# The norm's factor moved from in front of a feed-forward block to its gate and its result, in two of four blocks of a float32 transformer kernel

## What is computed

```python
def rms_norm(x, g, eps):
    xf = x.astype(jnp.float32)
    y = xf * lax.rsqrt(jnp.mean(xf * xf, axis=-1, keepdims=True) + eps)
    return (y * g.astype(jnp.float32)).astype(x.dtype)

def swiglu(h, w_gate_up, w_down):
    gu = h @ w_gate_up
    g, u = jnp.split(gu, 2, axis=-1)
    return (jax.nn.silu(g) * u) @ w_down

def second_block(...):
    for l in range(DEPTH):                       # DEPTH = 2
        ...
        x = x + rms_norm(m, norm_mix_post[l], NORM_EPS)
        h = rms_norm(x, norm_ffn_pre[l], NORM_EPS)
        f = swiglu(h, w_gate_up[l], w_down[l])
        x = x + rms_norm(f, norm_ffn_post[l], NORM_EPS)
```

## Time and profile before

| | |
|---|---|
| median of 3 runs | 4113.35 us (4108.27 to 4121.14) |
| the profiled execution, own time | 4109.69 us |
| its span | 4107.9 us |
| PE busy | 3872.9 us, 94% |
| DVE, ACT, POOL busy | 1541.3, 1503.3, 1261.4 us |
| mean granted TensorE clock | 0.973 of full |

### The profile page before, as it was taken

One profiled execution on the slowest core, in us unless ns is written; L12 is line 12 of the kernel. 1 busy time (PEld: TensorE's weight loads), 2 busy tenths in 40 slices (PEclk: granted clock), 3 DMA queues, 4 the chain that ended last, 5 costly groups with the idle time before them and its releaser, 6 DMA issues.

```text
span 4107.9 us, 59148 instructions
## 1 busy us (share of the span) xinstructions
PE 3872.9 (94%) x22684; PEld 3081.7 (75%) x22684; DVE 1541.3 (38%) x2360; ACT 1503.3 (37%) x2506; POOL 1261.4 (31%) x524
## 2 busy tenths in 40 slices
PE   6998999999986999999979999989998999998998
PEld 4875678888874777788857778868886777876886
DVE  2023454242423555353335555331115655323112
ACT  3324343121234444332245555232224555333222
POOL 2530042222221000244432323434442322343443
PEclk9999999999998999999999999999999999999999
DMA  4324621111120000122222122222221221222222
GB/s 179 114 93 147 243 88 62 62 62 62 62 67 31 16 15 20 67 87 97 97 73 67 62 67 72 97 68 97 97 97 62 67 67 62 79 94 74 98 93 87
DMA packets 84707, 333.87 MB, mean 81 GB/s; under 512 B 9520, under 2 KB 9648, under 8 KB 78000
## 3 DMA queue, kind: packets, MB, share of 16 engines
q1 hardware_dynamic: 83808, 329.22, 23.6%
q10 hardware_dynamic: 720, 2.10, 0.1%
HBM read 329.18 MB, written 2.10 MB: 81 GB/s over the span
## 4 chain that ended last, share of the span: by engine, by line
PE 62%; issue 26%; POOL 6%; DVE 3%; ACT 2%; POOLq 0%; DVEq 0%; ACTq 0%
PE pB L1903 13%; PE pB L276 12%; PE pB L278 12%; PE pB L277 12%; POOL w_lo L2423 6%; PE pO L1517 2%; PE pS L408 2%; PE pB L1499 1%; PE pS L1499 1%; PE pT L1509 1%; PE pS L1933 1%; PE pT L1961 1%; PE pO L1983 1%; PE pO L1988 1%; PE pS L1938 0%
## 5 line engine op out<-in xcount | busy, mean ns | idle before, releaser
L2423 POOL TENSOR_TENSOR w_lo<-w_raw,w_hi 128x1024 fp32r<-128x1024 f32 x520 | 1261.2, 2426 | 2819.7 <-ACT w_hi L314 2819.2
L276 PE MATMUL pB<-h_hi,w_hi 128*128 128x512 f32 x2080 | 825.8, 397 | 49.5 <-POOL w_lo L2423 17.3
L277 PE MATMUL pB<-h_lo,w_hi 128*128 128x512 f32 x2080 | 814.9, 392 | 0.0
L278 PE MATMUL pB<-h_hi,w_lo 128*128 128x512 f32 x2080 | 814.3, 391 | 0.0
L314 ACT ACTIVATE w_hi<-w_raw 128x1024 fp32r<-128x1024 f32 x520 | 547.9, 1054 | 500.6 <-PE pB L278 329.2
L276 PEld LDWEIGHTS pB<-h_hi,w_hi 128*128 128x128 f32 x2080 | 395.1, 190 | 140.9 <-issue 51.5
L277 PEld LDWEIGHTS pB<-h_lo,w_hi 128*128 128x128 f32 x2080 | 395.4, 190 | 84.0 <-issue 4.3
L278 PEld LDWEIGHTS pB<-h_hi,w_lo 128*128 128x128 f32 x2080 | 394.7, 190 | 83.2
L276 PE MATMUL pB<-b_hi,w_hi 128*128 128x512 f32 (+1 forms) x1120 | 425.1, 380 | 16.1 <-DVE xb_lo L685 10.3
L278 PE MATMUL pB<-b_hi,w_lo 128*128 128x512 f32 (+1 forms) x1120 | 411.6, 367 | 0.0
L277 PE MATMUL pB<-b_lo,w_hi 128*128 128x512 f32 (+1 forms) x1120 | 411.4, 367 | 0.0
(11 more groups left out here) (463 smaller groups left out, 5216.5 us busy)
## 6 DMA issues: line engine op xcount, KB each, us to landing
w_raw<-stream SPq DMA_DIRECT2D x520, 512.0 KB, 3.3
under<-ada SPq DMA_DIRECT2D x42, 1024.0 KB, 4.8
arena<-ada SPq DMA_DIRECT2D x6, 1024.0 KB, 18.8
x<-xT SPq DMA_DIRECT2D x1, 2048.0 KB, 9.9
out<-x SPq DMA_DIRECT2D x8, 256.0 KB, 2.0
xc<-cT SPq DMA_DIRECT2D x1, 1024.0 KB, 10.8
arena<-bmask ACTq DMA_DIRECT2D x1, 1024.0 KB, 5.1
arena<-brope ACTq DMA_DIRECT2D x2, 256.0 KB, 5.3
```

What stands on the lines that cost most here:

```text
L276: pe.matmul(dst, lh, rh, start=(begin and k == 0), stop=False)
L277: pe.matmul(dst, lh, rl, start=False, stop=False)
L278: last = pe.matmul(dst, ll, rh, start=False, stop=(end and k == len(pairs) - 1))
L2423: pool.tensor_tensor(w_lo[:, s, :], w_raw[:, s, :], w_hi[:, s, :].bitcast(F32), ALU.subtract).then_inc(lo_ready, 1)
```

## The change

In both layers of the second block:

- PE sums no squares ahead of the block. `pe_scaled_chunks` starts three chunks (it was two) as soon as the first tile of x times gain is there, and puts the sums of squares between the tiles: the sum of tile kt-1 ahead of the products of tile kt, the last two ahead of the products of tile 7.
- ACT (`act_scaled`) makes `h_hi` straight from x with the gain as scale, then squares the tile, for 8 tiles, then Ln and Exp. DVE (`dve_post_split`) makes `h_lo` from x, gain and `h_hi` two tiles behind `dve_post`'s own work. The norm's own three operations on a tile (lines 384, 353, 392) become two.
- Each gate is multiplied by `rstd` on DVE into `cbuf`, and ACT's Silu reads `cbuf` after it; ACT's order (Silu, then the high part of the third chunk ahead) is kept. In the block's first hidden tile that order puts the high part of chunk g+3 behind the Silu, and the Silu behind `rstd`.
- The finished `f` is multiplied by `rstd` on DVE in the last piece, before ACT squares it.

```diff
--- before.py
+++ after.py
@@ -696,11 +696,29 @@
                 items(dve, nj, SLOTS, body, j0)
                 items(dve, KD, SLOTS, out_body)
 
+        def pe_scaled_chunks(pe, g, name):
+
+            for e in range(SLOTS):
+                pe_wait_chunk(pe, g + e)
+            for kt in range(KD):
+                if kt:
+                    pe_square_sum(pe, name, kt - 1, T)
+                if kt == KD - 1:
+                    pe_square_sum(pe, name, kt, T)
+                pe.wait_ge(*normed(name)(kt))
+                for e in range(SLOTS):
+                    s = (g + e) % SLOTS
+                    last = pe_three(pe, bank[s][:, :], [(wt(s, kt), rows(*H, T, kt, 0, T))], kt == 0, kt == KD - 1)
+                    if kt == KD - 1:
+                        last.then_inc(chunk_done, 1)
+
         def pe_ffn(pe, call, norm, n, width, post=None):
             for p, (j0, nj) in enumerate(PIECES):
                 g0 = g_piece(call, p)
-                first = 0 if p else 2
-                if first:
+                first = 0 if p else 2 if post is None else SLOTS
+                if first and post is not None:
+                    pe_scaled_chunks(pe, g0, norm)
+                elif first:
                     pe_first_chunks(pe, g0, first, normed(norm), H, width, n)
                 items(pe, 2 * nj - first, SLOTS, lambda m: pe_chunk(pe, m + g0, H, width, n), first)
 
@@ -721,16 +739,16 @@
                     s = j % SLOTS
                     if not made:
                         act_hi_part(act, g + 2)
-                    act.wait_ge(chunk_done, done(g))
                     if conv:
+                        act.wait_ge(chunk_done, done(g))
                         act.wait_ge(conv_ready, v(j + (call * F_TILES + 1)))
                         act.activation(gpad[:, s, 1:1 + n], bank[g % SLOTS][:, 0:n], ACT.Copy).then_inc(evac[g % SLOTS], 1)
                         act_hi_part(act, g + 3)
                         act.wait_ge(conv_ready, v(j + (call * F_TILES + 1 + SLOTS)))
                         act.activation(cbuf[:, s, 0:n], cbuf[:, s, 0:n], ACT.Gelu_apprx_tanh).then_inc(gelu_ready, 1)
                     else:
-                        act.wait_ge(act_lo, v(j + (call * F_TILES + 1)))
-                        act.activation(cbuf[:, s, 0:n], bank[g % SLOTS][:, 0:n], ACT.Silu).then_inc(evac[g % SLOTS], 1)
+                        act.wait_ge(*ev(g))
+                        act.activation(cbuf[:, s, 0:n], cbuf[:, s, 0:n], ACT.Silu).then_inc(gelu_ready, 1)
                         act_hi_part(act, g + 3)
                     act.wait_ge(*ev(g + 1))
                     o = dyn(j - j0, T) if n == T else bass.ds(v((j - j0) * T), n)
@@ -766,7 +784,10 @@
                         dve.scalar_tensor_tensor(cj, gpad[:, s, 2:2 + n], w[2], cj, ALU.mult, ALU.add).then_inc(conv_ready, 1)
                         dve.wait_ge(gelu_ready, v(J + 1))
                     else:
-                        dve.wait_ge(*ev(g))
+                        dve.wait_ge(chunk_done, done(g))
+                        dve.wait_ge(act_lo, v(J + 1))
+                        dve.tensor_tensor(cbuf[:, s, 0:n], bank[g % SLOTS][:, 0:n], rstd, ALU.mult).then_inc(evac[g % SLOTS], 1)
+                        dve.wait_ge(gelu_ready, v(J + 1))
                     dve.wait_ge(chunk_done, done(g + 1))
                     dve.wait_ge(act_lo, v(J + 1))
                     dve.tensor_tensor(vbuf[:, s, 0:n], bank[(g + 1) % SLOTS][:, 0:n], cbuf[:, s, 0:n], ALU.mult).then_inc(evac[(g + 1) % SLOTS], 1)
@@ -785,14 +806,20 @@
                                          ALU.mult, ALU.add).then_inc(evac[(m + g0) % SLOTS], 1)
             return body
 
-        def f_body(dve):
+        f_whole = sem("f_whole")
+
+        def f_body(dve, l):
             def body(p, g0, m):
                 dve.wait_ge(chunk_done, done(m + g0))
                 fm = f[:, dyn(m, 1), :].rearrange("p a b -> p (a b)")
                 if p == 0:
                     dve.tensor_copy(fm, bank[(m + g0) % SLOTS][:, :]).then_inc(evac[(m + g0) % SLOTS], 1)
+                elif p + 1 < len(PIECES):
+                    dve.tensor_tensor(fm, bank[(m + g0) % SLOTS][:, :], fm, ALU.add).then_inc(evac[(m + g0) % SLOTS], 1)
                 else:
-                    dve.tensor_tensor(fm, bank[(m + g0) % SLOTS][:, :], fm, ALU.add).then_inc(evac[(m + g0) % SLOTS], 1)
+                    dve.tensor_tensor(fm, bank[(m + g0) % SLOTS][:, :], fm, ALU.add).then_inc(f_whole, 1)
+                    dve.wait_ge(f_whole, v(m + (l * KD + 1)))
+                    dve.tensor_tensor(fm, fm, rstd, ALU.mult).then_inc(evac[(m + g0) % SLOTS], 1)
             return body
 
         def g_ffn_end(call):
@@ -2365,6 +2392,39 @@
                     dve.wait_ge(nt_ready, N_BASE[c] + k + 1)
                     dve.tensor_tensor(x[:, k, :], x[:, k, :], nt[:, k % 3, :], ALU.add).then_inc(x_ready, 1)
 
+        def dve_post_split(dve, l):
+
+            c = NORMS.index(f"mixpost{l}")
+            pre = N_OUT[NORMS.index(f"ffnpre{l}")]
+            dve.wait_ge(rstd_ready, c + 1)
+            for kt in range(KD + 2):
+                if kt < KD:
+                    if kt >= 3:
+                        dve.wait_ge(x_ready, 2 * l * KD + kt - 2)
+                    dve.scalar_tensor_tensor(nt[:, kt % 3, :], f[:, kt, :], col("mix_post", l * KD + kt), rstd, ALU.mult, ALU.mult
+                                             ).then_inc(nt_ready, 1)
+                if 1 <= kt <= KD:
+                    k = kt - 1
+                    dve.wait_ge(nt_ready, N_BASE[c] + k + 1)
+                    dve.tensor_tensor(x[:, k, :], x[:, k, :], nt[:, k % 3, :], ALU.add).then_inc(x_ready, 1)
+                if kt >= 2:
+                    k = kt - 2
+                    dve.wait_ge(nhi_ready, pre + k + 1)
+                    o = slice(k * T, k * T + T)
+                    dve.scalar_tensor_tensor(h_lo[:, o], x[:, k, :], col("ffn_pre", l * KD + k), h_hi[:, o].bitcast(F32),
+                                             ALU.mult, ALU.subtract).then_inc(nlo_ready, 1)
+
+        def act_scaled(act, l):
+
+            name = f"ffnpre{l}"
+            act.preload_act_table_set(LN_EXP)
+            act.wait_ge(chunk_done, done(G_OUT[l] + KD - 1))
+            for kt in range(KD):
+                act.wait_ge(x_ready, 2 * l * KD + kt + 1)
+                act.activation(h_hi[:, kt * T:kt * T + T], x[:, kt, :], ACT.Identity, scale=col("ffn_pre", l * KD + kt)).then_inc(nhi_ready, 1)
+                act_square(act, name, kt, tile_of(x), T)
+            act_root(act, name, T)
+
         def tile_of(t_, n=T):
             return lambda kt: t_[:, kt, 0:n]
 
@@ -2468,7 +2528,6 @@
                 pe_pairs(pe, l)
                 pe_merge(pe, l)
                 pe_out_sums(pe, G_OUT[l], H, T, T, KD, lambda kt: (m_lo, l * KD + kt + 1), f"mixpost{l}")
-                pe_norm(pe, f"ffnpre{l}", T)
                 pe_ffn(pe, 2 + l, f"ffnpre{l}", T, T, f"ffnpost{l}")
 
         @block.scalar
@@ -2530,8 +2589,7 @@
                 act_out_squares(act, G_OUT[l], SLOTS, f"mixpost{l}", ft, T)
                 act_norm(act, f"mixpost{l}", ft, T, T, squares=False)
                 act_hi_part(act, G_FFN[2 + l] + 2)
-                act_norm(act, f"ffnpre{l}", xt, T, T, None, None, (*H, 0), done(G_OUT[l] + KD - 1),
-                         tile_ready=lambda kt: (x_ready, 2 * l * KD + kt + 1))
+                act_scaled(act, l)
                 act_ffn(act, 2 + l, T, False, f"ffnpost{l}")
                 act_norm(act, f"ffnpost{l}", ft, T, T, squares=False)
 
@@ -2615,9 +2673,10 @@
                 dve_pairs(dve, link, l)
                 dve_merge(dve, l)
                 dve_wout(dve, l)
-                dve_post(dve, f"mixpost{l}", l, "mix_post", 2 * l)
-                dve_norm(dve, f"ffnpre{l}", xt, T, T, gains("ffn_pre", l), None, (*H, 0))
-                dve_ffn(dve, 2 + l, T, False, None, f_body(dve))
+                dve_post_split(dve, l)
+                dve.wait_ge(rstd_ready, NORMS.index(f"ffnpre{l}") + 1)
+                dve_ffn(dve, 2 + l, T, False, None, f_body(dve, l))
+                dve.sem_inc(nt_ready, KD)
                 dve_post(dve, f"ffnpost{l}", l, "ffn_post", 2 * l + 1)
```

## The result

| | before | after |
|---|---|---|
| median of 20 runs each | 4111.77 us (4108.05 to 4121.14) | 4123.05 us (4118.87 to 4131.65) |
| after / before | | 1.0028, 95% interval 1.0021 to 1.0034 |
| profiled execution, own time | 4109.69 us | 4121.07 us |
| mean granted TensorE clock | 0.973 | 0.970 |
| PE, DVE, ACT, POOL busy | 3872.9, 1541.3, 1503.3, 1261.4 us | 3878.8, 1586.0, 1505.5, 1262.5 us |

The changed kernel is 11.3 us slower, 0.28%.

What follows compares the result with a forecast made beforehand. PE was taken to bound the kernel, standing at two seams for squares and low parts. Per layer +1.2 seam, +1.4 clock, +0.75 tail made +3.3, twice +6.7 us: 4116.4, or 4120.0 by median; forecast 4118, range 4104 to 4129.

Steps and rivals of the forecast that it cites:

- three signs of being wrong: Fourth chunk's high part before the Silu; stand costing the clock longer than 7 us; PE waiting for squares in last output chunks.
- First product: At each seam into the feed-forward block, PE's first product starts at about 2724.3, 12.4 us earlier than 2736.66.
- Tiles and sums: In the first three chunks, the first tile takes 3.84 us at half clock, later tiles with a sum 2.90 us.
- The queue behind the factor: From last sum to fourth chunk 7.8 us, PE standing 4.9 us; the fourth chunk starts 1.2 us later than before.
- The table load: Ahead of each seam's Silu, the load costs 1.28 us by the trace, without the skill's drain of about 1.38 us.
- The second clock loss: After PE's stand ahead of the fourth chunk, half clock probably follows, costing 1.4 us a layer, ends nothing and 2.9.
- The result's scaling: At each layer's end, the eighth tile's scaling has nothing behind it and puts 0.75 us on the path.
- the other seven fit: In each layer's last piece, scaling of seven result tiles is hidden, with 3.3 us of room for 0.7.
- The rival: Result scaling queues behind two back-to-back POOL operations, making squares 2.7 us late, 11 us in all, 4127 to 4131; chance 0.06.
- The gates' scaling: In steady hidden tiles, 0.69 us of DVE before each Silu is hidden; without cover it would cost 44 x 0.69.
- all that follows moves with it: From the fourth chunk on PE is dense, so only that chunk's start counts and everything later shifts with it.
- The second seam: The other layer's block boundary, 990 us later, has the same pattern as the first and counts as equal.

Runs made afterwards that it cites:

- e2: The changed kernel with two chunks instead of three in step ahead of the factor; median 4.8 us below before, ratio 0.9988.
- e1: The changed kernel with the fourth chunk's high part made ahead of the first hidden tile's Silu and table load; median 5.7 us above before, ratio 1.0009.
- e3: The changed kernel with 20 filler matmuls behind the third chunk, while PE stands for the fourth chunk's weights; median 4.5 us above before, ratio 1.0012.
- e10: e6 with the gate's scaling done twice on DVE in two of three hidden tiles; median 7.2 us below before, ratio 0.9983.
- e5: The changed kernel, unedited, run again in another job; median 9.1 us above before, ratio 1.0024.
- e4: The changed kernel without multiplying the finished result by the norm's factor; median 5.6 us above before, ratio 1.0014.
- e6: The changed kernel with two chunks in step and the finished result unscaled; median 8.9 us below before, ratio 0.9978.
- e7: e6 with 32 filler matmuls ahead of the block, while PE stands for the first new x tile; median 12.9 us below before, ratio 0.9968.
- e8: The kernel before, with 26 filler matmuls ahead of the feed-forward norm's sums and 15 behind them; median 1.8 us below before, ratio 0.9996.
- e9: e7 with 26 filler matmuls ahead of and 15 behind the sums of both mixers' norms; median 19.6 us below before, ratio 0.9945.
- e11: e9 with the omitted second factor multiplied in on DVE behind the Silu, in each hidden tile; median 19.5 us below before, ratio 0.9950.
- e12: e8 with 26 filler matmuls ahead of and 15 behind the sums of both mixers' norms; median 8.3 us below before, ratio 0.9980.

## Why the prediction came out as it did

Forecast 4118.0 with 4104 to 4129, "within 0.3%" at 0.83; measured 4123.05, ratio 1.0028. The kind and the sign of the mechanism were right. The size was 11.0 us where the sum had +6.7, and that the time still fell within 0.3% was close: the interval reaches 1.0034. None of the prediction's three signs of being wrong came, but the low clock at the stand, 6.8 us in all, was near its limit of 7.

- **First product.** Forecast 8.7 us behind the last sum (2724.3 against 2715.58), measured 8.69. The 12.4 us that were to be won were won.
- **Tiles and sums.** Forecast 3.84 for the first tile at half clock and 2.90 for the others; the sums stand 3.91 behind the first product and then 2.92 apart. From the first product to the fourth chunk 29.9 was forecast, and 30.1 measured.
- **The queue behind the factor.** Forecast 7.8 us from the last sum to the fourth chunk with a stand of 4.9; the stand is 4.68, and Ln, Exp, table load, Silu, high part and POOL come in this order. The net +1.2 a seam came out as +1.3. e2 and e1 show it from the other side.
- **The table load.** It starts at 2749.33, takes 1.28 and the Silu starts at 2750.63, as in the earlier trace rows. The rule of the Trainium skill (ScalarE: Activation LUTs, "What ACT_TABLE_LOAD costs"), with a drain of about 1.38 us for each switch, isn't borne out by this trace either; going by the row was right, by 2.8 us.
- **The second clock loss: the term that was mis-sized.** That a stand of 4.9 costs the clock was right. I gave it 1.4 us a layer, seven products at the half rate. e3 gives 2.0 for it by itself, and the change's trace some ten products, 4.4 us behind the fourth chunk's start where I had reckoned with 3. (The bill's 2.2 has 0.1 to 0.2 in it that isn't this loss.) Two layers: 1.2 to 1.6 too little.
- **The result's scaling.** Forecast 0.75 a layer on the path, measured 0.72 to 0.73 (PE's idle time ahead of the layer's last sum, 0.59 before, 1.31 after). That the other seven fit was right as well, though they are not as cheap as 0.69 while POOL works beside them: in layer 0 they take 1.92, 2.48, 2.14, 1.78, 1.42, 1.07 and 0.83 us, and the eighth 0.69.

```profile
3075.51 0.69 DVE L820 TENSOR_TENSOR arena<-pB,arena 128x512 f32 x1 [1.43 <-PE pB L278]
3075.77 2.40 POOL L2483 TENSOR_TENSOR w_lo<-w_raw,w_hi 128x1024 fp32r<-128x1024 f32 x1 [2.24 <-ACT w_hi L314]
3076.24 2.48 DVE L822 TENSOR_TENSOR arena<-arena,attA 128x512 f32 x1
...
3080.18 1.02 PE L408 MATMUL pS<-attT,cm 128*128 128x512 f32 x2
```

  The addition that reads PSUM takes 0.69, the scaling that reads SBUF alone takes 2.48 and ends 0.55 behind POOL. PE's sums stay 4.98 us apart all the same (3075.20, 3080.18, on to 3105.07). The rival needed two POOL operations back to back, and there is one.
- **The gates' scaling** is hidden, as forecast; e10 shows it.
- **The step that failed: "all that follows moves with it".** The second seam has the pattern of the first, as forecast (38.79 us). But what lies between the seams doesn't just move, and the prediction had put it at nothing without a row. Layer 1's norm and mixer, whose instructions the diff leaves alone, take 2.5 us longer (+1.07, +1.38), with the clock at half speed for longer in the same places. In after, e2 and e5 it is 21.64 and 583.6, in before, e4, e6 and e10 it is 20.57 and 582.2 to 582.3. All of the first three scale the result, none of the others does; e1 and e3, which scale it too, lie between (21.26 and 583.30, 20.94 and 582.76). But e7, which doesn't scale it, takes 21.16 and 580.31, so the scaling as such isn't the cause.

The last point is where the rest went. What tells the profiles apart is where the clock falls behind layer 0's last sum. Where it falls 4.1 us behind it (before, e4, e6, e10) or 4.6 (e8), it is back after 6.8 us. Where it falls sooner (3.4 us in after, e5 and e2, 2.6 in e1, 2.4 in e7, 1.9 in e3), it stays low for 10.2 us, and the norm takes 0.4 to 1.1 us more. Scaling the result puts the last sum 0.7 us later and so closer to the fall (4.1 in e4 and 3.4 in the change, which differ by the scaling alone; 4.1 in e6 and 3.4 in e2). A seam of another length shifts it as well, as in e7. Why the fall comes where it comes no run tells. The Trainium skill (TensorE: Matmul & The Clock Gate, "What's actually happening") says that the gate looks at activity in windows that run free of the kernel, so that the place of a transition shifts from run to run. That a shift of under 1 us decides how much is lost fits with such windows. The shifting from run to run isn't seen here: two profiles of the same program (after, e5) lost the same to about 0.02 us, and layer 0's mixer took 582.46 to 582.53 us in all eleven profiles without filler in front of it, with the clock low in the same places. Delaying layer 1 by other amounts with the same work would have told more; it wasn't tried.

## What to carry to other kernels

Moving a factor out of the way frees the engine ahead of it, but count how much work is left to run over the chain that now stands behind it: here three chunks ending together left none and the kernel lost 11 us; with two in step, and nothing else changed, it gained 2.7 by the distance and 4.8 by the median. A factor is cheapest where another engine has slack in every iteration (28 more operations on the gates, and 44 more behind the Silu, cost nothing), and dearest at an end that nothing covers (the last one, of 0.7 us, cost all of it). And each stand of TensorE is to be priced with the slow products behind it: here 2.0 us a seam, where the later start itself cost 1.3.

## What the runs showed of the hardware that I had not expected

- Matmuls into an unread bank during a stand kept the granted clock at 1.00 and delayed what came next by 0.04 to 0.13 us. That was worth 2.0 us a seam in e3 and 1.6 to 1.7 in e7.
- What they change isn't only beside them. With 26 and 15 of them at the start of layer 0's mixer, falls of the clock 219 and 318 us behind its first product are absent, and the mixer is 5.7 to 5.9 us shorter, about half of it by these two falls (e9, e11, e12). Before, PE stood for 1.34 us in all in the 4 us ahead of each fall. In e12 the same work with the same 1.34 us of idling (2441 to 2445, the row above) is not followed by a fall, so the stand alone doesn't decide it. Whether the added activity does, or that all behind it comes some us earlier, is not shown.
- Where the sums of squares waited for ACT, the same clock was worth only 0.4 us a seam (e8).
